# One block in front of the feed-forward: the last three tiles of the attention's output projection by halves, and all rows of half 0 updated and squared under them

## The reference

```python
y = windowed_gqa_sink(h, att_w_qkv[j], att_w_o[j], att_sink[j], rel_bias)   # ends with out @ w_o
x = x + g1 * rmsnorm(y, mix_norm_post[i])
h = rmsnorm(x, ffn_norm_pre[i]) * (1.0 + sc2) + sh2
y = swiglu(h, ffn_w_in[i], ffn_w_out[i])
```

## Time and profile before

| | us |
|---|---|
| median of three runs | 2924.6 |
| lowest and highest | 2921.72, 2927.68 |
| the profiled execution, and its span | 2927.36, 2925.6 |
| PE busy | 2801.6 (96%) |
| DVE busy | 1845.2 (63%) |
| ACT busy | 1285.9 (44%) |
| POOL busy | 440.7 (15%) |

### The profile page before, as it was taken

The page is one execution under the profiler, slowest core; times in us unless marked ns, Lnnn a source line. Parts: engine busy times, 40 slices in busy tenths (PEclk is TensorE's granted clock), DMA queues, the critical chain, the costliest instruction groups (busy, mean ns, idle before and its releaser), DMA issues. The chain is left out here.

```text
span 2925.6 us, 37705 instructions
## 1 busy us (share of the span) xinstructions
PE 2801.6 (96%) x14123; PEld 2265.7 (77%) x14123; DVE 1845.2 (63%) x2990; ACT 1285.9 (44%) x2032; POOL 440.7 (15%) x258
## 2 busy tenths in 40 slices
PE   7999998999999999899999999999999998999999
PEld 4766675778887778577988888888878767888886
DVE  6365787778778577836555122544431348999997
ACT  4355634542223243434444212222211236999995
POOL 1000020000000000011000222212122112544443
PEclk9999999999999999999999999999999998999999
DMA  6000064564445757323101212110222225777774
GB/s 254 30 23 16 9 246 156 188 221 163 165 145 195 285 195 283 132 103 113 33 24 62 78 70 102 43 44 34 102 72 75 104 103 214 262 269 267 257 264 169
DMA packets 116407, 407.32 MB, mean 139 GB/s; under 512 B 23556, under 2 KB 29988, under 8 KB 104736
## 3 DMA queue, kind: packets, MB, share of 16 engines
q1 hardware_dynamic: 82104, 348.82, 32.6%
q10 hardware_dynamic: 16440, 39.98, 3.7%
q0 software_dynamic: 17712, 16.52, 2.6%
HBM read 402.05 MB, written 82.66 MB: 166 GB/s over the span
## 5 line engine op out<-in xcount | busy, mean ns | idle before, releaser
L662 PE MATMUL psum<-ff_g,ffo_w_split 128*128 128x512 f32 x1056 | 247.2, 395 | 10.4 <-POOLq L799 5.9
L662 PEld LDWEIGHTS psum<-ff_g,ffo_w_split 128*128 128x128 f32 x1056 | 199.5, 190 | 53.6 <-POOLq L568 6.3
L4239 DVE TENSOR_TENSOR ex_g_lo<-ex_g_raw,ex_g_hi 128x1024 fp32r<-128x1024 f32 x188 | 221.0, 1217 | 0.8 <-ACT ex_g_hi L4176 0.7
L1045 PE MATMUL psum<-fi_t_sum_hi,fi_w_sum 128*128 128x512 f32 x704 | 220.3, 389 | 0.0
L4176 ACT CAST ex_g_hi<-ex_g_raw 128x1024 fp32r<-128x1024 f32 x188 | 192.0, 1053 | 1.5 <-PE psum L4119 1.5
L1045 PEld LDWEIGHTS psum<-fi_t_sum_hi,fi_w_sum 128*128 128x128 f32 x704 | 132.2, 188 | 27.4
L4117 PE MATMUL psum<-ex_g_hi,ex_x_hi 128*128 128x512 f32 x376 | 150.9, 401 | 0.0
L4119 PE MATMUL psum<-ex_g_hi,ex_x_lo 128*128 128x512 f32 x376 | 147.1, 391 | 0.0
L4118 PE MATMUL psum<-ex_g_lo,ex_x_hi 128*128 128x512 f32 x376 | 147.1, 391 | 0.0
L1045 PE MATMUL psum<-fi_t_sum_lo,fi_w_sum 128*128 128x512 f32 x352 | 137.1, 389 | 0.0
L1104 ACT CAST fi_w_sum<-fi_sum 128x512 fp32r<-128x512 f32 x88 | 54.4, 622 | 173.7 <-PE psum L1045 105.9
(11 more groups left out here) (659 smaller groups left out, 7561.0 us busy)
## 6 DMA issues: line engine op xcount, KB each, us to landing
ex_g_raw<-in_w_experts_gu_dram SPq DMA_DIRECT2D x32, 2048.0 KB, 8.5
ex_d_raw<-in_w_experts_d_dram SPq DMA_DIRECT2D x32, 1024.0 KB, 8.6
fi_raw<-in_ffn_in_dram SPq DMA_DIRECT2D x22, 1024.0 KB, 5.3
ffo_w_raw<-in_ffn_out_dram SPq DMA_DIRECT2D x31, 704.0 KB, 6.3
wom_w<-in_mod_w_dram SPq DMA_DIRECT2D x8, 2048.0 KB, 8.1
fi_first_raw<-in_ffn_in_dram SPq DMA_DIRECT2D x22, 512.0 KB, 4.5
ff_g<-fi_g SPq DMA_DIRECT2D x43, 256.0 KB, 2.0
ml_raw<-in_w_ml_dram SPq DMA_DIRECT2D x16, 512.0 KB, 5.1
```

The source lines that it names most:

```text
L662: mm = nc.tensor.matmul(chip.psum[:, 2 * u + h, :], w[:, v % 2, k * P:(k + 1) * P], (a[u] if isinstance(a, tuple) else a)[:, c * n_kc + k, ...
L1045: mm = mm_(self.result(name, j), w[:, part, k * P:(k + 1) * P], a[:, k, :], start=(k == 0 and p3 == 0), stop=(k == 3 and p3 == 2))
L4239: nc.vector.tensor_tensor(cols(g_lo, n), cols(raw.g_raw[i % 3], n), cols(g_hi, n).bitcast(F32), ALU.subtract).then_inc(q["g_lo_made"], 1)
```

## The change

Six edits, all between the head of the `wo` block and the first gate products.

- Tiles 5, 6 and 7 run by halves, in the order 5, 6, 7 (half 0), 6, 7, 5 (half 1). Two slots can't keep three tiles, so tile 5's weights are loaded and split a second time for its half 1.
- The square sum of half 0 is made after three rows of the fourth half step, as a sum of `att_acc` and of the last square tile.
- All eight rows of half 0 are updated in the block; ACT squares each, and PE sums the eight squares between the products and after them. Root and reciprocal (`first_rstd`) are the last instructions of ACT and DVE.
- `x` comes in four loads of 1 MB beside the first weight loads. SP's list is written out anew for the whole block.
- The three squares of half 1 that are left are added by three more float32 products at the head of the next block.
- The next block begins with the scaling of row 0; the updates, squares and the reciprocal for half 0 are gone from it, and ACT starts with the casts of the first gate weights.

```diff
@@ gemm, SP @@
-            if ready:
+            if last_tiles:
+                for s in range(n_m + 1):
+                    if s >= ready:
+                        load(s, s % 2, last_tiles.TILE_AGAIN if s == n_m else s)
+                    if 1 <= s <= 4:
+                        last_tiles.load_x(sp, s - 1)
+                    if s < n_m - 1:
+                        on_sp(sp, s // 2, s % 2)
+                on_sp(sp, n_m // 2 - 1, 1)
+            elif ready:
                 loaded_body()
                 body_behind_loaded()
...
@@ LastTiles @@
+    TILE_AGAIN = 5
+    STEPS = ((5, 0, 5), (6, 0, 6), (7, 0, 7), (6, 1, 6), (7, 1, 7), (5, 1, 8))
+    DONE = KD - 3
...
+        def sum_first():
+            pe.wait_ge(self.added, self.DONE + 4)
+            pe.matmul(chip.psum[:, FirstRows.SUMS, :], chip.ones[:], self.acc[:, self.part(0)], start=True, stop=False)
+            pe.wait_ge(self.squared, self.DONE + 4)
+            pe.matmul(chip.psum[:, FirstRows.SUMS, :], chip.ones[:], self.sq[2], start=False, stop=True).then_inc(self.summed, 1)
+
+        def sum_square(k):
+            pe.wait_ge(self.x_squared, k + 1)
+            pe.matmul(chip.psum[:, FirstRows.SQUARES, :], chip.ones[:], self.x_sq[k % 4][:], start=(k == 0), stop=(k == KD - 1))\
+                .then_inc(self.x_used if k < KD - 1 else self.x_summed, 1)
+
+        for i, (m, h, p) in enumerate(self.STEPS):
+            pe.wait_ge(lo_made, p + 3)
+            pe.wait_ge(self.copied, (6, 6, 7, 7, 8, 9)[i])
+            for k in range(KD):
+                if (i, k) == (3, 3):
+                    sum_first()
...
+                if i == 5 and k % 2 == 1:
+                    sum_square(2 + k // 2)
+            if i < 4:
+                self.beside.turn(pe, 4 + i, i % 2)
+            if i == 4:
+                sum_square(0)
+                sum_square(1)
+        sum_square(KD - 2)
+        sum_square(KD - 1)
...
+        split(6, (self.squared, self.DONE + 1))
+        split(7, (self.half_used, 1))
+        evacuate(0)
+        evacuate(1)
+        evacuate(2)
+        act.wait_ge(self.summed, 1)
+        nc.scalar.activation(self.rstd[:], chip.psum[:, FirstRows.SUMS, :], ACT.Sqrt, scale=1.0 / D, bias=chip.eps[:, 0:1])\
+            .then_inc(self.root, 1)
+        split(8, (self.half_used, 4))
+        evacuate(3)
+        square(0)
+        square(1)
+        square(2)
+        evacuate(4)
+        for k in range(3, KD):
+            square(k)
+        evacuate(5)
+        act.wait_ge(self.x_summed, 1)
...
-        for k in range(self.early.FIRST_ROWS):
-            dve.wait_ge(self.copied, k + 3)
+        for k in range(KD):
+            dve.wait_ge(self.x_in[k // 2], 16)
...
+        dve.wait_ge(self.x_root, 1)
+        v.reciprocal(self.early.rstd[:], self.early.rstd[:])
@@ Sevenths, PE @@
-        mm_(chip.psum[:, 2, :], chip.ones[:], self.y_acc[:, HALF:S], start=True, stop=True).then_inc(q["y_summed"], 1)
-        for k in range(KD):
-            pe.wait_ge(q["squared"], k + 1)
-            mm_(chip.psum[:, 3, :], chip.ones[:], self.sq[k % 2][:], start=(k == 0), stop=(k == KD - 1)).then_inc(q["used"], 1)
+        mm_(chip.psum[:, 2, :], chip.ones[:], self.y_acc[:, HALF:S], start=True, stop=False)
+        for n, squares in enumerate(self.first.left):
+            mm = mm_(chip.psum[:, 2, :], chip.ones[:], squares, start=False, stop=(n == 2))
+        mm.then_inc(q["y_summed"], 1)
@@ Sevenths, ACT @@
-        for k in range(KD):
-            act.wait_ge(q["x_new"], k + 1)
-            if k >= 2:
-                act.wait_ge(q["used"], k - 1)
-            act.activation(self.sq[k % 2][:], self.x(k, 0), ACT.Square).then_inc(q["squared"], 1)
...
+        for n in range(4):
+            first_hi(n)
+        act.wait_ge(q["y_summed"], 1)
+        act.activation(self.rstd_y[1][:], chip.psum[:, 2, :], ACT.Sqrt, scale=1.0 / D, bias=chip.eps[:, 0:1]).then_inc(q["y_root"], 1)
         for k in range(KD):
             full(k, 0, KD + k + 1)
```

More of the change, by code:

```diff
@@ new lines, in __init__ @@
+        self.x_in = [chip.sem(f"{name}_x_in{u}") for u in range(4)]
+        self.half_used, self.summed, self.root, self.inverted, self.mod_made, self.coef_made, self.t_made, self.x_new, self.x_squared, \
+            self.x_used, self.x_summed, self.x_root = \
+            (chip.sem(f"{name}_last_{x}") for x in ("half_used", "summed", "root", "inverted", "mod_made", "coef_made", "t_made", "x_new",
+                                                    "x_squared", "x_used", "x_summed", "x_root"))
@@ L714, in part @@
     def part(self, h):
         return slice(h * HALF, (h + 1) * HALF)
[L717 to L727, removed]
-        nc, chip = self.nc, self.chip
[L729 to L744, removed]
+    def load_x(self, sp, u):
+        sp.dma_start(self.chip.x[:, 2 * u:2 * u + 2, :], self.x_dram[:, 2 * u:2 * u + 2, :]).then_inc(self.x_in[u], 16)
+    def on_pe(self, pe, w_hi, w_lo, hi, lo, lo_made):
+        chip = self.chip
+        def sum_first():
[13 more added lines that the diff above has]
+                    sum_first()
+                for p3, (w, a) in enumerate(((w_hi, hi), (w_hi, lo), (w_lo, hi))):
+                    mm = pe.matmul(chip.psum[:, (2, 3, 0, 1, 2, 3)[i], :], w[:, p % 2, k * P:(k + 1) * P], a[:, k, self.part(h)],
+                                   start=(k == 0 and p3 == 0), stop=(k == KD - 1 and p3 == 2))
+                if k == KD - 1:
+                    mm.then_inc(self.half_used, 1)
+                if i == 5 and k % 2 == 1:
[7 more added lines that the diff above has]
+        sum_square(KD - 1)
@@ new lines, in on_act, with split, evacuate, square @@
+    def on_act(self, act, w_raw, w_hi, w_in, hi_made):
+        nc, chip = self.nc, self.chip
+        def split(p, until):
+            act.wait_ge(w_in[p % 2], 16 * (p // 2 + 1))
+            act.wait_ge(*until)
+            nc.scalar.copy(w_hi[:, p % 2, :], w_raw[:, p % 2, :]).then_inc(hi_made, 1)
+        def evacuate(i):
+            m, h, _ = self.STEPS[i]
+            bank = chip.psum[:, (2, 3, 0, 1, 2, 3)[i], :]
+            act.wait_ge(self.half_used, i + 1)
+            act.wait_ge(self.added, self.DONE + (1, 2, 3, 2, 3, 4)[i])
+            nc.scalar.activation(self.sq[i], bank, ACT.Square).then_inc(self.squared, 1)
+            nc.scalar.copy(self.y[:, m, self.part(h)], bank).then_inc(self.copied, 1)
+        def square(k):
+            act.wait_ge(self.x_new, k + 1)
+            if k >= 4:
+                act.wait_ge(self.x_used, k - 3)
+            nc.scalar.activation(self.x_sq[k % 4][:], self.early.x(k, 0), ACT.Square).then_inc(self.x_squared, 1)
+        split(6, (self.squared, self.DONE + 1))
[16 more added lines that the diff above has]
+        act.wait_ge(self.x_summed, 1)
+        nc.scalar.activation(self.early.rstd[:], chip.psum[:, FirstRows.SQUARES, :], ACT.Sqrt, scale=1.0 / D, bias=chip.eps[:, 0:1])\
+            .then_inc(self.x_root, 1)
@@ L746, in on_dve, with add @@
     def on_dve(self, dve):
         v, chip, beside = self.nc.vector, self.chip, self.beside
[L748 to L753, removed]
+        def add(n, part, sq):
+            dve.wait_ge(self.squared, n)
+            dve.wait_ge(self.added, n)
+            v.tensor_tensor(self.acc[:, part], self.acc[:, part], sq, ALU.add).then_inc(self.added, 1)
@@ L754, in on_dve @@
+        add(self.DONE + 1, slice(0, S), self.tile_sq[:])
+        beside.on_dve(v, 2, 1)
+        add(self.DONE + 2, self.part(0), self.sq[0])
+        beside.on_dve(v, 3, 0)
+        add(self.DONE + 3, self.part(0), self.sq[1])
+        beside.on_dve(v, 3, 1)
         dve.wait_ge(self.root, 1)
@@ L814, in end_pe @@
     def end_pe(pe):
-        if beside and not last_pair:
+        if beside and not last_tiles:
             beside.end_pe(pe)
```

118 lines of the change are left out of this document (49 added, 69 removed).

## The result

The changed kernel took 2932.9 us (median of 8 runs, 2930.5 to 2936.9), the kernel before 2925.1 (8 runs, 2920.7 to 2928.8). The ratio is 1.0025, with a 95% interval of 1.0016 to 1.0033: slower by 4.7 to 9.7 us. The forecast was 2931.1, or +6.5. That the change is slower is clear; that it is slower by over 0.2%, the bound that the prediction names, is not, since the interval begins at 0.16%.

A forecast was written before the change was run, and what follows sets the result against it. TensorE, 96% busy, was taken as the bound, except at the seam, set by a chain of rows. Head +6.0, sums +9.0, seam 23.6 cut to 15.1: +6.5 us on 2924.6, forecast 2931.1; 8-in-10 range 2924.5 to 2934.5.

The forecast's parts named there:

- tile 1's weights rounded, from ACT's first rounding: Head of the `wo` block: tile 1's weights, issued behind `wom_w`, land at 382.9, and ACT stands 5.5 us.
- row 4's remainder late for PE: Head of the `wo` block: PE gets row 4's remainder 4.5 us late, bounds 3.0 to 5.1.
- second stretch at half clock: Head of the `wo` block: after two PE waits the clock halves a second time, costing 1.5 us (0 to 1.7).
- head together: Head of the `wo` block: late remainder and half clock together cost 6.0 us (3.0 to 6.8).
- sums in the block, to PE's end: In the `wo` block: nine added fp32 products at 1.0 us each cost PE 9.0 us (8.6 to 9.9).
- block's start to first gate product: Head of the feed-forward block: loads, casts, root and row 0 on ACT put the first gate product at +9.6 us.
- first gate product later by: Start of the feed-forward products: first gate product at 502.9 against 496.44, moving the end by +6.5 us.
- The first: Head of the `wo` block: tile 1's weights arrive early and are not held up; -6.0 us, 2925.1; chance 0.12.
- the second: Head: clock falls no second time, or GpSimd does not hold DVE; head 4.5 or less, 2928 to 2929.7; chance 0.27.
- the third: In the `wo` block: updates come late, up to 2.4 us, half-1 sums add 0.7; up to 2934; chance 0.12.
- The fourth: New seam: without casts before row 0, row 0 sets the start at +3; -6.6 us, 2924.5; no separate chance given.
- The rows after it keep order and pace: Behind the first gate product: nothing further is gained or lost, so the end moves by the same +6.5 us.

The follow-up runs named there:

- e1: The changed kernel with SP again issuing tile 1's and tile 2's weights ahead of the first and second modulation steps; 2927.9 us, ratio 1.0004 to the kernel before.
- e2: The kernel before with one edit: SP issues the first modulation step (2 MB) ahead of tile 1's weights; 2934.3 us, ratio 1.0023 to the kernel before.
- e6: The changed kernel with two runs of nine unread products filling PE's two waits for row 4 in tile 0; 2932.4 us, ratio 1.0019 to the kernel before.
- e3: The changed kernel with ACT making rows 0 and 1 before the gate-weight casts, DVE's first weight remainders behind row 1; 2933.2 us, ratio 1.0017 to the kernel before.
- e4: The changed kernel with SP's old order, two gate weights loaded before the barrier, row 0 after two casts, two half-1 sums later; 2922.5 us, ratio 0.9987.
- e9: The changed kernel with ACT issuing the first modulation step (2 MB) on its own queue, tile 1's weights first on SP's; 2933.9 us, ratio 1.0025.
- e5: The changed kernel with each of the eight half-0 squares of x summed twice on PE, the copy unread; 2939.6 us, ratio 1.0044 to the kernel before.

## Why the prediction came out right, and where its terms were off

The sum was made of steps, and the trace has a number for each, counted from the start of the block.

| step | forecast us | measured us |
|---|---|---|
| tile 1's weights rounded, from ACT's first rounding | 9.3 | 9.26 |
| row 4's remainder late for PE | 4.5 | 4.35 |
| second stretch at half clock | 1.5 (0 to 1.7) | 2.6 |
| head together | 6.0 (3.0 to 6.8) | 6.9 |
| sums in the block, to PE's end | 9.0 (8.6 to 9.9) | 8.7 |
| root and reciprocal; barrier | 4.1; 1.4 | 4.1; 1.4 |
| block's start to first gate product | 9.6 | 9.95 |
| first gate product later by | 6.5 | 7.5 |

- **Head.** The mechanism and its place were right, and e1 and e2 show that it alone decides the sign: without it the change is within 0.13% of no change. Row 4's remainder is late by 4.35 (386.48 - 372.60 against 383.09 - 373.56). The mis-sized term is the clock: bounded at 1.7 from the one stretch that the kernel before shows, it cost 2.6 (7.76 us from that product to ACT's square, 5.19 before), since the half clock lasted 5 us instead of 3. e6 gave 2.4 of it back.
- **Sums.** The nine were taken at 1.0 each and cost 0.86 each, 7.7; a wait of 0.53 for the modulation's turn, which had not been counted, is part of the other 1.0. No sum of squares waited for its square.
- **Seam.** The first weights landed 5.0 and 6.2 us into the block, not 4.1 and 5.8. Perhaps x's store slows them, which now follows them on SP's queue sooner; that was not tried. (The forecast's own terms, 7.5 + 0.6 + 0.85 + 0.62 + 0.14, add up to 9.7, not 9.6.) The forecast that ACT's queue behind these loads, not the row chain, sets the start is shown by e3 and e4.
- **Rivals.** The first (tile 1 not held up) failed by the cast at 381.86; the second by the granted clock of 0.50, and in its other half by row 4's remainder, which came near the 4.5 late that was counted with GpSimd in DVE's way, not 3.0; the third by PE's sums, which waited for nothing. The fourth is what e4 builds.
- **What was missed.** "The rows after it keep order and pace" was not so: from the first gate product to the first product of the next stage the change took 133.1 us (503.0 to 636.1), the kernel before 136.0 (496.4 to 632.4). The first products of the next stage (tile view, before and in the change; the two numbers behind the durations are first and last start), and the waits for half 1's sum among the gate products, before, in the change and in e1:

```profile
L1045 PE MATMUL psum<-fi_t_sum_hi,fi_w_sum x704: 388/390/390, 632.4 to 928.7; 128*128 128x512 f32 x176
L1108 PE MATMUL psum<-fi_t_sum_hi,fi_w_sum x704: 389/389/389, 636.1 to 932.3; 128*128 128x512 f32 x176
```

```profile
PE psum L1066 <- DVE fi_sq_sum L1367: 5.1, 1, 5.1
```

```profile
PE psum L1129 <- DVE fi_sq_sum L1421: 4.0, 1, 4.0
```

```profile
PE psum L1131 <- DVE fi_sq_sum L1423: 4.0, 1, 4.0
```

In these two executions part of the loss was given back, and the wait is 1.1 us shorter. That PE comes 7 us later is not what shortens it: in e1 the first gate product comes as early as before (122.6 us from the start of the `wo` block, 122.9 before), and its wait is 4.0 too. The cause and the size stay open: e2, with the old order of this block, took 135.6, and the profiled executions with the new one 132.6 to 136.5. The later stages vary by some 4 us from one execution to another, and so does each profile's span; the timed ratio, not the spans, says that 4.7 to 9.7 us were lost. So the steps up to the first gate product are borne out by the trace, each within 1.1 us. That what lies behind it came out near nothing, as the forecast had it, no run here tells from luck.

## What to carry to other kernels

When a list of transfers is written anew, look up for each small transfer which large one now stands ahead of it, and what is queued in program order behind its reader. When work that covered a block's first loads is moved away, move the loads as well, into space that is free before the barrier. And price a wait of TensorE by what its clock does afterwards too: here 4.0 us of waiting cost 2.6 more at half clock.

## What the runs showed of the hardware

- In e9 two queues shared the DMA engines by packets, not by bytes: 45 packets of 4 KB against 40 of 16 KB in 2 us. A 512 KB load beside a 2 MB load took 8.2 us on its own queue, against 8.7 behind it in the same one (373.20 to 381.86 in the change), and with nothing ahead of it at most 3.6 in the kernel before and 4.1 in e1 (373.52 to 377.65).
- Eighteen products that nobody reads, in waits of 2.2 and 1.8 us, kept the granted clock at 1.00 behind row 4's remainder, where the change had 5 us at 0.50, and made the head 2.4 us shorter (e6).
- A row sum in float32 (128x512, two products in the trace) costs 0.86 us at full clock (e5), and 1.84 for the first after a pause (493.00 to 494.84 in the change), where the granted clock was 0.50.
